# The order of the matmuls inside a unit: blocks outermost, or thirds of the tokens outermost

## What is computed

```python
for layer in range(DEPTH):                    # DEPTH = 2
    hn = rms_norm(h, mix_norm_gain[layer])
    if layer % 2 == 0:                        # Fourier features and grouped attention
        h = h + fourier_attention_mixer(hn, ab_w_in[j], ..., ab_w_out[j], cos, sin)
    else:                                     # gated linear recurrence, 8 heads, two directions
        h = h + hgrn2_mixer(hn, c_w_in[j], lower_bounds[layer], c_o_gain[j], c_w_out[j])
    h = h + sq_relu_mlp(rms_norm(h, mlp_norm_gain[layer]), mlp_w1[layer], mlp_w2[layer])
return rms_norm(h, final_norm_gain)[:, N_META:]
```

## Time and profile before

| | |
|---|---|
| median of three executions | 3066.51 us (3064.62 to 3066.75) |
| span of the profiled execution, first to last instruction | 3063.7 us |
| mean granted TensorE clock over the span | 0.973 of full |
| TensorE matmul busy | 2885.9 us, 94% of the span |
| VectorE, ScalarE, GpSimd busy | 49%, 23%, 30% |
| HBM traffic | 38 GB/s over the span |

### The profile page before, as it was taken

How to read it: one execution, slowest core, us unless ns; L and a number is a source line. 1 busy time by engine, 2 the same in 40 slices (tenths; PEclk the granted TensorE clock), 3 DMA queues, 4 the chain that set the end, 5 groups by cost and what they waited for, 6 DMA issues and landing times.

```text
span 3063.7 us, 44165 instructions
## 1 busy us (share of the span) xinstructions
PE 2885.9 (94%) x18229; PEld 2809.6 (92%) x18229; DVE 1498.5 (49%) x1832; ACT 692.8 (23%) x968; POOL 922.2 (30%) x396
## 2 busy tenths in 40 slices
PE   7998999999999999999899899999769999999998
PEld 6897999999999999998898898888659999999998
DVE  6377885432222222446866866767744222222224
ACT  3117883211000111112122222132232011100012
POOL 2130003344334434332222222222103434434432
PEclk9998999999999999999999999999879999999999
DMA  4010001111111111110000000000001111111111
GB/s 143 28 35 1 0 0 35 42 49 49 42 49 45 46 49 46 44 49 28 28 28 27 27 26 29 21 27 28 19 9 42 42 49 49 42 49 49 42 49 69
DMA packets 169465, 117.25 MB, mean 38 GB/s; under 512 B 3714, under 2 KB 163796, under 8 KB 169334
## 3 DMA queue, kind: packets, MB, share of 16 engines
q1 hardware_dynamic: 169190, 114.70, 12.3%
q10 hardware_dynamic: 144, 0.53, 0.1%
HBM read 111.03 MB, written 4.19 MB: 38 GB/s over the span
## 4 chain that ended last, share of the span: by engine, by line
PE 79%; DVE 13%; issue 5%; ACT 2%; DMA 0%; SPq 0%; DVEq 0%; ACTq 0%
PE ps L1180 67%; PE ps L1306 3%; PE ps L1445 3%; PE ps L1400 2%; DVE aa L1013 1%; DVE h L912 1%; DVE kk L1033 1%; PE ps L1468 1%; DVE kk L1032 1%; PE ps L1412 1%; ACT prob L565 1%; DVE ssq L768 1%; PE ps L1256 1%; DVE fd L1040 1%; DVE qq L1036 1%
## 5 line engine op out<-in xcount | busy, mean ns | idle before, releaser
L1180 PE MATMUL ps<-xh,wsp 128*128 128x348 f32 x5568 | 1074.6, 325 | 20.9 <-DVE xl L762 12.6
L461 POOL TENSOR_TENSOR wsp<-raw,ones 128x1024 fp32r<-128x1024 f32 x196 | 389.0, 1984 | 2087.2 <-PE ps L1180 2069.0
L1180 PEld LDWEIGHTS ps<-xh,wsp 128*128 128x128 f32 x5568 | 919.7, 190 | 27.8 <-issue 22.3
L1180 PE MATMUL ps<-xl,wsp 128*128 128x348 f32 x2784 | 596.1, 323 | 0.0
L1180 PE MATMUL ps<-ah,wsp 128*128 128x348 f32 x3072 | 574.3, 321 | 0.0
L463 POOL TENSOR_TENSOR wsp<-raw,wsp 128x1024 fp32r<-128x1024 f32 x196 | 533.1, 2720 | 15.3
L1180 PEld LDWEIGHTS ps<-ah,wsp 128*128 128x128 f32 x3072 | 503.6, 188 | 0.0
L912 DVE TENSOR_TENSOR h<-h,ps 128x1044 f32<-128x1044 f32 x200 | 246.9, 1240 | 512.1 <-PE ps L1180 510.5
L1180 PEld LDWEIGHTS ps<-xl,wsp 128*128 128x128 f32 x2784 | 474.2, 189 | 0.0
L925 DVE SCALAR_TENSOR_TENSOR tmp<-ps,rms 128x1044 f32<-128x1044 f32 x64 | 79.8, 1246 | 556.9 <-PE ps L1180 551.2
L1180 PE MATMUL ps<-al,wsp 128*128 128x348 f32 x1536 | 326.5, 321 | 0.0
(11 more groups left out here) (179 smaller groups left out, 2835.8 us busy)
## 6 DMA issues: line engine op xcount, KB each, us to landing
raw<-in_w SPq DMA_DIRECT2D x128, 512.0 KB, 3.8
raw<-in_c_w_in SPq DMA_DIRECT2D x40, 512.0 KB, 3.8
raw<-in_ab_w_in SPq DMA_DIRECT2D x12, 512.0 KB, 3.8
xst<-in_x SPq DMA_DIRECT2D x8, 512.0 KB, 6.4
raw<-in_ab_w_out SPq DMA_DIRECT2D x8, 512.0 KB, 3.7
raw<-in_c_w_out SPq DMA_DIRECT2D x8, 512.0 KB, 3.4
out<-ost SPq DMA_DIRECT2D x16, 256.0 KB, 3.0
tabs<-in_dft_tok SPq DMA_DIRECT2D x2, 856.4 KB
```

The source lines that it names most:

```text
L461: nc.gpsimd.tensor_tensor(wsp[:, slot, 0, :], raw[:, slot, :], one, ALU.mult).then_inc(w_high, 1)
L1180: ins = M(ps[:, 3 * s + c, 0:CB], w(a, k), b(k)[:, c * CB:(c + 1) * CB], start=(k == first and a == 0 and b is xa), stop=(k == last and a ...
```

## The change

In `blocks`, when there is no `ready` function, the loop over the thirds becomes the outermost: for a third, all blocks of input features and all three terms go in a row into its one bank, then the next third. With a `ready` function the order stays. Nothing is added or taken away: the matmuls are the same, the sums in each bank are formed in the same order, and the first matmul of a unit still raises `w_used` and the last `z_ready`. In a unit that is cut by a gap, each piece goes through the three thirds by itself.

```diff
-                for k in ks:
-                    if ready is not None:
+                def product(k, a, b, c):
+                    return M(ps[:, 3 * s + c, 0:CB], w(a, k), b(k)[:, c * CB:(c + 1) * CB],
+                             start=(k == first and a == 0 and b is xa), stop=(k == last and a == 1))
+
+                terms = ((0, xa), (0, xb), (1, xa))
+                if ready is not None:
+                    for k in ks:
                         ready(k)
-                    for a, b in ((0, xa), (0, xb), (1, xa)):
-                        for c in range(3):
-                            ins = M(ps[:, 3 * s + c, 0:CB], w(a, k), b(k)[:, c * CB:(c + 1) * CB],
-                                    start=(k == first and a == 0 and b is xa), stop=(k == last and a == 1))
+                        for a, b in terms:
+                            for c in range(3):
+                                ins = product(k, a, b, c)
+                                if opens:
+                                    ins.then_inc(w_used, 1)
+                                    opens = False
+                    return ins
+                for c in range(3):
+                    for k in ks:
+                        for a, b in terms:
+                            ins = product(k, a, b, c)
                             if opens:
                                 ins.then_inc(w_used, 1)
                                 opens = False
```

## The result

The changed kernel takes 3070.20 us (median of 13, 3063.39 to 3074.70) against 3062.76 us for the kernel before, now also from 13 executions (3059.33 to 3070.26). The ratio is 1.0020, with a 95% interval of 1.0013 to 1.0028. In a second series on another occasion the ratio was 1.0014 (1.0005 to 1.0023). By them the change costs 6.1 us in the first series and 4.3 us in the second: at the edge of what I had called "no change", and on the slower side of it.

What follows compares the result with a forecast made beforehand. TensorE's matmul line 1180 was taken as the bound: 13752 matmuls x (159.1 - 159.0) ns = +1.4 us, taken as zero, with waits unchanged, giving 3066.5 us, range 3060 to 3073 us.

Steps and rivals of the forecast that it cites:

- no change: Whole kernel: a measured time within 0.2%, 6.1 us, of the time before; chance 0.86.
- What bounds the kernel: Whole kernel: TensorE has a matmul for 94% of the span, so line 1180's start-to-start time, 159.0 ns, decides.
- The bank and the weights: Line 1180: 24 matmuls in a row into one bank, 6 weight changes in 9 instead of 2; expected free.
- slower rival: Every unit: bank additions or weight changes raise the distance to 160.0 ns, +13.8 us, ending at 3080 us; chance 0.07.
- The moving operand: Line 1180's activations: one piece each of high, low, high instead of three neighbouring pieces; 159.1 against 159.0 ns, +1.4 us.
- The uncertainty of the pitch: Line 1180's start-to-start time before, 159.0 ns, was given 0.3 ns (4.1 us) of uncertainty from the choice of stretch.
- The bounds: Attention stretch halves: eight score distances gave -0.8 ns (-11 us), nine value distances +1.0 ns (+13.8 us) per matmul.
- The level of the kernel before: Whole kernel: the median before was taken as 3066.5 us, the profiled span as 3063.7 us.
- Clock and eviction: Two faster rivals: recurrent mixer's clock held up, 3038 us, chance 0.01; earlier eviction of thirds, 3026 us at best, 0.01.
- What would show it wrong: Both MLPs: a distance of 159.5 ns or more, or 158.5 or less; or releases a third of a unit earlier or later.

Runs made afterwards that it cites:

- high_high_low: Changed kernel with a block's terms ordered high x high, low x high, high x low; 3067.70 us, 1.0014 of the kernel before.
- terms_outside: Changed kernel with, inside each third, the terms outside the blocks of input features; 3070.68 us, 1.0023 of the kernel before.

## Why the prediction was wrong, point by point

- **What bounds the kernel** was right: 94% of the span, no wait of any size moved, and the difference that is clear of noise is in the start-to-start time of one line, which my first part had named as the only thing that counts.
- **The bank and the weights**, the two mechanisms of my slower rival, cost nothing (1.0000 and 1.0001, distances unchanged to 0.01 ns). That rival had the right sign, by causes that the runs rule out. That the bank costs nothing carried over from nine in a row, as I had read it in the attention, to 24.
- **The moving operand** is the step that failed. I listed it as the third difference and then took the attention as its stand-in, "which is the new order of `blocks`": 158.8 ns, corrected to 159.1. The kind of sequence is the same, but the addresses are others, and the addresses decide. Seventeen distances at one place in SBUF say nothing on 72 distances at another. More of them would not have helped: all 839 undisturbed distances of the attention in the same trace have a mean of 158.9 ns, 159.2 with the same correction, and the first product went to 159.5. The term was +0.1 ns (+1.4 us, rounded to zero) and measured +0.29 ns (+4.0 us): +0.6 in the MLP's first product, +0.2 in its second, and -0.25 in the attention's output product (159.11 to 158.86).
- **The uncertainty of the pitch** was misread. I took the difference of the earlier trace rows, 159.0 and 158.7 ns, for scatter of 0.3 ns, within which a change could hide. In truth each value is exact: 158.70 ns is what one slot of the MLP's second product takes in every pass, and the other takes 159.27. The variation by place was the signal: it said that the addresses matter. The same holds for "three in 0.48, six in 0.94", which I used only against a cost of the weights.
- **The bounds**, -0.8 to +1.0 ns from the two halves of the attention stretch, held the measured +0.29 ns; the central value did not. The range 3060 to 3073 us held 3070.2 us, which the next point shows to be luck, and 0.86 for a move below 0.2% was too much for a term known to 0.3 ns, when 0.45 ns decides.
- **The level of the kernel before** was 3062.8 us in 13 executions instead of 3066.5 us in three. The range's centre stood 4 us too high, which hid part of the rise: around 3062.8 us a range of the same width would end at 3069 us and miss.
- **Clock and eviction**: no gain, as expected. The granted clock is 1.00 and 0.94 in the two stretches shown, and TensorE's wait for the additions is 33.9 us instead of 33.4.
- **What would show it wrong** was well chosen for the first product (159.5 ns or more: 159.54) and not reached in the second (159.17).

## What to carry to other kernels

Where a stream of matmuls fills an engine, read the start-to-start time over long stretches of each stage and compare it with columns over clock: here 145.0 ns of 159.0 are columns, and in a stream without stops only the rest was touched by the order. Measure with the same tiles at the same addresses; a piece of the trace with the same loop nest but other addresses misses effects of half a nanosecond, which are 0.2% of the kernel. A change of 0.2% in a kernel of this kind is not yet a property of the new order, since moving the tiles by 64 bytes does as much to the old one. Within this kernel the new order even helps in one of two slots and costs in the other. The tempting reasons, banks and weight changes, can be tested alone with kernels that compute the wrong thing at the right pace.

## What the runs showed of the hardware

- A float32r matmul with its weight load costs its columns plus 28 to 48 cycles of 2.4 GHz, mostly 32 to 36, at 256 to 384 columns (118.7 to 176.7 ns). At the low clock this constant is not seen: the three matmuls of the earlier trace rows, at a granted clock of 0.50, are 290 ns apart, and 348 columns at 1.2 GHz are 290.0 ns.
- The start-to-start time depends on the sequence of activation addresses: up to 174 ns against 159 in single positions, and 158.55 (`high_high_low`) to 160.02 ns (`terms_outside`) in the mean of a pass. The mean repeats for shifts of 1024 and 2048 bytes but not of 32 or 64.
- It locks: the same matmul repeated settles at one value, and for 352 columns at 158.4 or 166.7 ns in different rounds of the same loop.
- Neither adding 24 times in a row to one bank nor the real changes of the weights between matmuls cost anything: 158.91 ns against 158.90.
